# Holding weight blocks instead of activation blocks in the feed-forward gate and up products of a fused transformer kernel

## The reference, cut to what matters

```
D_FF = 2816
def swiglu(x, w_gate, w_up, w_down):
    return (jax.nn.silu(x @ w_gate) * (x @ w_up)) @ w_down
for l in range(DEPTH):                       # DEPTH = 2
    x = layer_norm_2(ALPHA * x + 0.5 * swiglu(x, ffn1_gate[l], ffn1_up[l], ffn1_down[l]), ln1_g[l], ln1_b[l])
    ...                                      # the mixer and its norm
    x = layer_norm_2(ALPHA * x + 0.5 * swiglu(x, ffn2_gate[l], ffn2_up[l], ffn2_down[l]), ln3_g[l], ln3_b[l])
```

## Time and profile before

| what | value |
|---|---|
| median of the three executions | 1748.15 us |
| the profiled execution | 1752.66 us |
| its span, first to last instruction | 1750.9 us |
| granted TensorE clock, mean | 0.99 |
| TensorE matmuls busy | 1700.0 us (97%), 8422 instructions |
| TensorE weight loads busy | 1240.2 us (71%), 8422 instructions |
| VectorE busy | 878.5 us (50%) |
| ScalarE busy | 674.5 us (39%) |

### The profile page before, as it was taken

The page is one execution under the profiler, slowest core; times in us unless marked ns, Lnnn a source line. Parts: engine busy times, 40 slices in busy tenths (PEclk is TensorE's granted clock), DMA queues, the critical chain, the costliest instruction groups (busy, mean ns, idle before and its releaser), DMA issues.

```text
span 1750.9 us, 20133 instructions
## 1 busy us (share of the span) xinstructions
PE 1700.0 (97%) x8422; PEld 1240.2 (71%) x8422; DVE 878.5 (50%) x1158; ACT 674.5 (39%) x924; POOL 101.5 (6%) x97
## 2 busy tenths in 40 slices
PE   9999998889999988989999999999999999999998
PEld 7774443359864434378888888888888888888886
DVE  5572111167771211275456676555655457775445
ACT  6442111146621111154433754444444336744432
POOL 1020000010000000000003002000200021020000
PEclk9999999999999999999999999999999999999999
DMA  9558999994469999955556426554656557255551
GB/s 350 179 213 348 422 420 421 421 320 149 141 270 417 421 418 421 402 177 192 180 181 203 158 96 220 184 191 169 221 188 192 173 166 231 97 192 192 178 172 60
DMA packets 142624, 426.50 MB, mean 244 GB/s; under 512 B 7592, under 2 KB 20144, under 8 KB 117952
## 3 DMA queue, kind: packets, MB, share of 16 engines
q1 hardware_dynamic: 136720, 407.00, 63.1%
q0 software_dynamic: 5808, 18.17, 3.3%
HBM read 424.08 MB, written 1.06 MB: 243 GB/s over the span
## 4 chain that ended last, share of the span: by engine, by line
PE 88%; DMA 6%; DVE 3%; ACT 1%; issue 0%; SPq 0%; POOL 0%; DVEq 0%
PE ps L569 19%; PE ps L561 17%; PE ps L564 17%; PE ps L1756 15%; DMA whole<-in_moe_w_up 5%; PE ps L691 2%; PE ps L553 2%; PE ps L1709 2%; PE ps L554 2%; PE ps L1821 2%; PE ps L2713 1%; DMA whole<-in_moe_w_down 1%; PE ps L2614 1%; PE ps L671 1%; PE ps L670 1%; PE ps L669 1%
## 5 line engine op out<-in xcount | busy, mean ns | idle before, releaser
L497 DVE TENSOR_TENSOR Wlo<-raw,Whi 128x2048 fp32r<-128x2048 f32 (+3 forms) x199 | 435.9, 2197 | 355.7 <-ACT Whi L486 355.4
L486 ACT ACTIVATE Whi<-raw 128x2048 fp32r<-128x2048 f32 (+3 forms) x205 | 375.8, 1842 | 375.5 <-PE ps L569 370.9
L569 PE MATMUL ps<-Whi,XTl 128*128 128x512 f32 (+2 forms) x1208 | 445.2, 384 | 0.0
L561 PE MATMUL ps<-Whi,XTh 128*128 128x512 f32 (+2 forms) x1048 | 408.1, 389 | 0.2 <-DVE XTl L703 0.2
L564 PE MATMUL ps<-Wlo,XTh 128*128 128x512 f32 (+2 forms) x1048 | 403.6, 385 | 0.0
L569 PEld LDWEIGHTS ps<-Whi,XTl 128*128 128x128 f32 x1208 | 225.6, 189 | 43.7
L1756 PE MATMUL ps<-whole,p_XG 128*64 128x512 f32 (+2 forms) x992 | 233.5, 610 | 12.0 <-DMA whole<-in_moe_w_up 9.3
L561 PEld LDWEIGHTS ps<-Whi,XTh 128*128 128x128 f32 x1048 | 197.4, 188 | 40.2 <-issue 3.1
L564 PEld LDWEIGHTS ps<-Wlo,XTh 128*128 128x128 f32 x1048 | 197.5, 188 | 37.1 <-issue 0.2
L1756 PEld LDWEIGHTS ps<-whole,p_XG 128*64 128x64 f32 (+2 forms) x992 | 75.0, 139 | 148.1 <-issue 146.8
L1933 DVE TENSOR_TENSOR Ygl<-ps,Ygh 128x512 fp32r<-128x512 f32 x32 | 22.1, 692 | 234.1 <-ACT Ygh L1888 234.1
(11 more groups left out here) (363 smaller groups left out, 1756.9 us busy)
## 6 DMA issues: line engine op xcount, KB each, us to landing
whole<-in_moe_w_up SPq DMA_DIRECT2D x64, 1024.0 KB, 13.6
whole<-in_moe_w_down SPq DMA_DIRECT2D x64, 1024.0 KB, 14.8
whole<-in_moe_w_gate SPq DMA_DIRECT2D x60, 1024.0 KB, 13.4
raw<-in_ffn_gate SPq DMA_DIRECT2D x40, 1024.0 KB, 5.1
raw<-in_ffn_up SPq DMA_DIRECT2D x40, 1024.0 KB, 5.0
raw<-in_ffn_down SPq DMA_DIRECT2D x40, 1024.0 KB, 5.1
raw<-in_w_in SPq DMA_DIRECT2D x18, 1024.0 KB, 6.1
raw<-in_a_w_in SPq DMA_DIRECT2D x10, 1024.0 KB, 15.0
```

The costliest lines, as they stand in the source:

```text
L486: act.activation(Whi[:, hi_at[i], 0:m * n], raw[:, raw_at[i], 0:m * n], ACT.Copy).then_inc(w_rounded, tick(w_rounded, "rounded", i))
L497: dve.tensor_tensor(Wlo[:, raw_at[i], 0:m * n], raw[:, raw_at[i], 0:m * n], h.bitcast(f32), ALU.subtract).then_inc(w_rest, tick(w_rest, "r ...
L561: pe.matmul(o, xh(k, t), h[:, q, :], start=k == first, stop=False)
L569: x = pe.matmul(o, xl(k, t), h[:, q, :], start=False, stop=k == end)
```

## The change

Chunk 0 is left as it is. In chunks 1 to 4 and in `fboth`, blocks of 128 x 128 weights become stationary and x of both token tiles streams past them, 256 columns to a matmul. The product comes out turned: feed-forward columns on the partitions, tokens along the row. One PSUM bank takes two blocks of 128 feed-forward columns by 256 tokens (index j), and the two banks of a job (index s, where t was) take the four. In `fboth` bank 0 is the gate and bank 1 the up. What VectorE multiplies is then already the layout of `hTh`, so for chunks 1 to 5 the transposes are gone, and ScalarE and VectorE split `hd` straight from SBUF.

```
+    def held_block(pe, o, h, l, k, first, end):
+        pe.matmul(o, h, XTh[:, k, :], start=first, stop=False)
+        pe.matmul(o, h, XTl[:, k, :], start=False, stop=False)
+        return pe.matmul(o, l, XTh[:, k, :], start=False, stop=end)
+
+    def job_held_pe(pe, name):
+        bs = [bank(pe, name, s, hold=True, at_once=s == 0) for s in range(2)]
+        for z, i in enumerate(jobs[name]):
+            _, m, n, k0, nk = units[i]
+            h, l = halves(i)
+            pe.wait_ge(*on("rest", i))
+            for s in range(2):
+                enter(pe, name, s)
+                for j in range(2):
+                    o, c = PS[bs[s]][:, j * 256:j * 256 + 256], slice(256 * s + 128 * j, 256 * s + 128 * j + 128)
+                    for q in range(m):
+                        x = held_block(pe, o, h[:, q, c], l[:, q, c], k0 + q, j == 0 and k0 + q == 0, j == 1 and k0 + q == nk - 1)
+                x.then_inc(unit_used, tick(unit_used, "used", i))
+                point[("prod", i, s)] = point[("used", i)]
+            if i == jobs[name][-1]:
+                release(*bs)
+            yield z
...
@@ ffn_pe
-        for c in range(5):
-            ...job_pe(pe, ("fgate", a, l, c), xt_h, xt_l, ready, ...)
-                if c > 0 and z == 0:
-                    turn(c - 1)
-            for z in job_pe(pe, ("fup", a, l, c), xt_h, xt_l, ready):
-                pass
-        for z in job_pe(pe, ("fboth", a, l), xt_h, xt_l, ready):
-            if z == 0:
-                turn(4)
+        for c in range(1, 5):
+            for z in job_held_pe(pe, ("fgate", a, l, c)):
+                if c == 1 and z == 0:
+                    turn()
+            for z in job_held_pe(pe, ("fup", a, l, c)):
+                pass
+        for z in job_held_pe(pe, ("fboth", a, l)):
+            pass
         for z in job_pe(pe, ("fdown", a, l, 0), ht_h, ht_l, h_ready):
-            if z == 0:
-                turn(5)
+            pass
@@ ffn_act
+                else:
+                    act.wait_ge(*on("hd", a, l, c, t))
+                    act.activation(hTh[:, 4 * c + 2 * t:4 * c + 2 * t + 2, :].rearrange("p k n -> p (k n)"), hd[:, t, :],
+                                   ACT.Copy).then_inc(act_done, tick(act_done, "hi", *name))
@@ ffn_dve
+                else:
+                    k = slice(4 * c + 2 * t, 4 * c + 2 * t + 2)
+                    dve.wait_ge(*on("hi", *name))
+                    dve.tensor_tensor(hTl[:, k, :].rearrange("p k n -> p (k n)"), hd[:, t, :],
+                                      hTh[:, k, :].rearrange("p k n -> p (k n)").bitcast(f32), ALU.subtract).then_inc(
+                        dve_done, tick(dve_done, "lo", *name))
...
+                if c > 1:
+                    dve.wait_ge(*on("lo", "hT", a, l, c - 1, s))
+                dve.scalar_tensor_tensor(hd[:, s, :], sg[:, s, :], 0.5, PS[b][:, :], ALU.mult,
+                                         ALU.mult).then_inc(dve_done, tick(dve_done, "hd", a, l, c, s))
```

More of the change, by code:

```diff
@@ L935, in ffn_pe, with turn @@
         ready = x_ready(v - 1)
-        def turn(c):
+        def turn():
             for t in range(2):
-                pe.wait_ge(*on("hd", a, l, c, t))
-                n = (CH[c][1] - CH[c][0]) // 128
-                turn_pe(pe, ("hT", a, l, c, t), [hd[:, t, k * 128:(k + 1) * 128] for k in range(n)])
+                pe.wait_ge(*on("hd", a, l, 0, t))
+                turn_pe(pe, ("hT", a, l, 0, t), [hd[:, t, k * 128:(k + 1) * 128] for k in range(4)])
         def h_ready(pe, k, t):
-            pe.wait_ge(*on("lo", "hT", a, l, k // 4, t))
-        for c in range(5):
-            second = (lambda: second_pe(pe, v - 1)) if c == 0 else None
-            for z in job_pe(pe, ("fgate", a, l, c), xt_h, xt_l, ready, skew=c == 0, second=second,
-                            early=x_early(v - 1) if c == 0 else None):
-                if c > 0 and z == 0:
-                    turn(c - 1)
-            for z in job_pe(pe, ("fup", a, l, c), xt_h, xt_l, ready):
-                pass
-        for z in job_pe(pe, ("fboth", a, l), xt_h, xt_l, ready):
-            if z == 0:
-                turn(4)
+            c = k // 4
+            pe.wait_ge(*on("lo", "hT", a, l, c, t if c == 0 else k % 4 // 2))
+        second = lambda: second_pe(pe, v - 1)
+        for z in job_pe(pe, ("fgate", a, l, 0), xt_h, xt_l, ready, skew=True, second=second, early=x_early(v - 1)):
+            pass
+        for z in job_pe(pe, ("fup", a, l, 0), xt_h, xt_l, ready):
+            pass
[4 more added lines that the diff above has]
+            for z in job_held_pe(pe, ("fup", a, l, c)):
+                pass
+        for z in job_held_pe(pe, ("fboth", a, l)):
+            pass
         for z in job_pe(pe, ("fdown", a, l, 0), ht_h, ht_l, h_ready):
-            if z == 0:
-                turn(5)
+            pass
         turn_0 = (lambda: x_turn_pe(pe, v, 0)) if split else None
@@ L964, in turn @@
         def turn(c):
-            for t in range(2):
-                n, name = (CH[c][1] - CH[c][0]) // 128, ("hT", a, l, c, t)
-                split_act(act, name, hTh[cols(CH[c][0] // 128, n, t)], turned(name, n))
+            for t in range(2 if c < 5 else 1):
+                name = ("hT", a, l, c, t)
+                if c == 0:
+                    split_act(act, name, hTh[cols(0, 4, t)], turned(name, 4))
+                else:
+                    act.wait_ge(*on("hd", a, l, c, t))
+                    act.activation(hTh[:, 4 * c + 2 * t:4 * c + 2 * t + 2, :].rearrange("p k n -> p (k n)"), hd[:, t, :],
+                                   ACT.Copy).then_inc(act_done, tick(act_done, "hi", *name))
         for c in range(6):
-            n, name = CH[c][1] - CH[c][0], ("fgate", a, l, c) if c < 5 else ("fboth", a, l)
+            name = ("fgate", a, l, c) if c < 5 else ("fboth", a, l)
             def gate(t, b):
+                if (c, t) == (5, 1):
+                    return
                 act.wait_ge(*product(name, t))
@@ L974, in gate @@
                     act.wait_ge(*on("hd", a, l, c - 1, t))
-                act.activation(sg[:, t, 0:n], PS[b][:, 0:n], ACT.Silu).then_inc(
+                act.activation(sg[:, t, :], PS[b][:, :], ACT.Silu).then_inc(
                     act_done, tick(act_done, "sg", a, l, c, t))
-                if c < 5:
-                    free(act_done, name, t)
+                free(act_done, name, t)
             for z in job_act(act, name, gate, skew=c == 0):
@@ L999, in turn @@
         def turn(c):
[L1000 to L1003, removed]
+            for t in range(2 if c < 5 else 1):
+                name = ("hT", a, l, c, t)
+                if c == 0:
+                    s = cols(0, 4, t)
+                    split_dve(dve, name, hTl[s], turned(name, 4), hTh[s])
+                else:
[4 more added lines that the diff above has]
+                        dve_done, tick(dve_done, "lo", *name))
         for c in range(6):
-            n, name = CH[c][1] - CH[c][0], ("fup", a, l, c) if c < 5 else ("fboth", a, l)
+            name = ("fup", a, l, c) if c < 5 else ("fboth", a, l)
             def up(t, b):
-                dve.wait_ge(*on("sg", a, l, c, t))
+                if (c, t) == (5, 0):
+                    return
+                s = t if c < 5 else 0
+                dve.wait_ge(*on("sg", a, l, c, s))
                 dve.wait_ge(*product(name, t))
-                src = PS[b][:, 0:n] if c < 5 else PS[b][:, 512 - n:512]
-                dve.scalar_tensor_tensor(hd[:, t, 0:n], sg[:, t, 0:n], 0.5, src, ALU.mult,
-                                         ALU.mult).then_inc(dve_done, tick(dve_done, "hd", a, l, c, t))
+                if c > 1:
+                    dve.wait_ge(*on("lo", "hT", a, l, c - 1, s))
+                dve.scalar_tensor_tensor(hd[:, s, :], sg[:, s, :], 0.5, PS[b][:, :], ALU.mult,
+                                         ALU.mult).then_inc(dve_done, tick(dve_done, "hd", a, l, c, s))
                 free(dve_done, name, t)
```

## The result

| | before | after |
|---|---|---|
| median | 1749.82 us (11 runs, 1747.78 to 1752.68) | 1756.72 us (11 runs, 1753.73 to 1758.26) |
| ratio | 1 | 1.0036, 95% interval 1.0028 to 1.0045 |
| the profiled execution | 1752.66 us, span 1750.9 | 1757.17 us, span 1755.4 |

What follows compares the result with a forecast made beforehand. The prediction took TensorE's own stream as the bound: +23.1 us of matmuls less 16.6 us of transposes made +6.5 us, on the median of 1748.15 us a forecast of 1754.7 us (+0.37%), range 1750.5 to 1759.5 us.

Steps and rivals of the forecast that it cites:

- The bound: In the feed-forward blocks a microsecond of TensorE's own stream is a microsecond of the kernel; other engines' work is free with slack.
- Exchange, +23.1 us: In the 72 changed units, 1728 matmuls of 512 columns (391.6 us) become 3456 of 256 (414.7 us).
- Transposes, -16.6 us: 144 of 176 transposes of `hd` go: 0.91 us per block of eight, 0.50 per four, over four feed-forward blocks.
- The sum: Matmuls' +23.1 us less transposes' 16.6 us gives +6.5 us on the whole kernel; the profiled execution was to take 1759.2 us.
- rival 4: Same mechanism, smaller size: held pitch 0.1196 us or scatter leaves the time within about 0.3%, 1751 to 1753.3 us; 26 in 100.
- ScalarE and VectorE, 0: Splitting `hd` from SBUF and the new product wait stay beside TensorE: 0, bounds -0.5 to +0.5 us.
- the slack for one delay (12 us): VectorE's rests of the weights are made ahead; only a delay above some 12 us would reach TensorE.
- The page's formula: Skill page's gap of N/2.4 + 2.5 ns per matmul: doubling would add 4.3 us, not 23.1; total 1735.9 us.
- Rival 2: Fixed part near nothing in the held stream: weight loads hide, only transposes' 16.6 us go, 1731.6 us; 3 in 100.
- rival 3: Each held unit starts with a restart of 0.18 us: 13 us on top over 72 units, 1767.7 us; 6 in 100.
- The least held step: Lower end for the step between held 256-column matmuls: 0.1133 us, half the 512 step, making the exchange 0.

Runs made afterwards that it cites:

- e1: The kernel before, with each 512-column matmul of the 72 touched units cut into two of 256, x still held, transposes kept: 1772.18 us, ratio 1.0119.
- e4: The changed kernel with x high and x low streamed as one 512-column matmul, VectorE adding the halves: 1740.58 us, ratio 0.9941 to before.
- e5: The changed kernel with the two token tiles streamed one after the other, 128 columns to a matmul, 96 a unit: 2113.24 us, ratio 1.2078 to before.
- e6: The kernel of e4 with VectorE making each addition of the two halves twice: 1757.87 us, ratio 1.0046 to before.
- e3: The changed kernel with the 144 transposes put back at their old places as idle work nobody reads: 1770.84 us, ratio 1.0106 to before.
- e2: The changed kernel with the three passes reordered so no two neighbours inside a block share their held block: 1756.50 us, ratio 1.0031 to before.

## Why the prediction was right

**The bound** (TensorE's own stream, nothing beside it). Right: the chain and the waits after are those of before, and the time of e1 to e4 followed their count and widths of matmuls; e5 needed another price for its width, and in e6 VectorE came in.

**Exchange, +23.1 us.** Right. The held step is 0.1201 us where 0.1200 was taken from the attention stage. Alone, in e1, it measures 22 us by the medians (the interval of the ratio is 17 to 25).

**Transposes, -16.6 us.** Right, with the size as the stream before pays it. In the stream after, a block costs 0.86 in place of 0.91 us (e1, e3); that touches the one block that stays, 0.05 us a feed-forward block.

**The sum.** From the first turning to the end of the span the two traces differ by 975.58 - 969.35 = 6.23 us, and the first changed unit ahead of it took 5.76 in place of 5.44: 6.55 us, forecast 6.5. The profiled execution after was 1757.17 us and not 1759.2, because it came to the changed part 2.05 us earlier (774.06 against 781.55 - 5.44 = 776.11 us). Nothing is changed ahead of that point; the same turning lies anywhere from 777.7 to 782.1 us in the kernels of the table (e5 aside, whose first changed unit is 5 us longer). That scatter, and one of 1 to 2 us in the mixers, is why single executions say little about 6 us. Over eleven executions each the interval of the ratio is clear of 1, but it begins at 1.0028, just inside the 0.3% that the prediction took as what can be told from no change. So the time alone doesn't rule out the smaller size of rival 4; the trace speaks for the forecast one, with a step of 0.1200 to 0.1201 us, not 0.1196.

**ScalarE and VectorE, 0.** Right for the change. The rest from SBUF costs what it did from PSUM, and chunk 5's is ready at 889.2 us, 17 us ahead of its use. But I reckoned the slack for one delay (12 us) and not for a delay that comes back in every chunk: in e6 3 us a chunk add up to 9 us over the three chunks ahead of the row at 871.67 us (the same row stands at 795.98), and only then do 2.1 us reach TensorE.

**The page's formula against the rows.** By N/2.4 + 2.5 ns of the Trainium skill, page "TensorE: Matmul & The Clock Gate", section "Back-to-back issue gap", the exchange would have cost 4.3 us, an estimate. The section gives that formula for a matmul by itself, and for a stream with weight loads about 81 ns at 128 columns and about 131 ns at 512, more than the formula at the one width and less at the other. The runs agree with neither: 22 us in e1, and steps of 0.1117, 0.1201 and 0.2266 us at 128, 256 and 512 columns. Rival 2 falls with it, and so does rival 3: 816 matmuls in one stream over 17 units, and no restart but the one behind the turning.

**One argument was right in its use and too wide in its words.** From 256, 280 and 512 columns I concluded that the step is columns plus a constant and that no fixed length of a load sets the 0.12. That holds from 256 columns up. Below, e5 shows a floor of 0.112 us. The least held step that I named, 0.1133 us, was half of the 512 step. At 256 columns it held as a bound, but halving doesn't carry on: half of 0.1201 is 0.060 us, and 128 columns took 0.1117.

## What to carry to other kernels

Where TensorE's stream is the bound, price a change of who is held by matmuls and not by columns: here each costs its columns at 2.4 GHz plus 13.4 ns from 256 columns up, and 0.112 us at 128, so 256 columns are a bad width to double the count for and 128 a ruinous one. Saved transposes are cheap (0.91 us for eight with their restart) and do not pay for 96 extra matmuls a chunk (1.3 us); look first whether two passes share the held operand and can stream as one, which turned +6.5 us into -9. Work given to another engine is free only while that engine's list, its waits for third engines included, is shorter than TensorE's for the same chunk: here at 75% load, and no more at 87%, where it took 25.2 us against 22.2. Being late costs more than the wait where the clock falls behind it.

## What the runs showed of the hardware that was not expected

The floor: 0.1117 us a step for 128-column float32 matmuls with a load each, 93% of the 0.1201 us for twice the columns (e5). And a repeated stationary block has its own load in the trace and saves no time at all (e1; e2: a stretch of 98.79 us against 98.78). And a wait of 2.1 us in an otherwise full stream was followed by 3.4 us at half clock in three cases of four (e6).
